# Depthwise convolution of a streaming encoder: products summed by accumulating transfers and turned one chunk later

## The reference

```
hn = rmsnorm(h, norm_mix[0])
u = hn @ w1 + b1;  a, gate = split(u);  u = a * sigmoid(gate)
u = causal depthwise conv(u, w_dw, width 31) + b_dw        # per channel, over positions
u = silu(layernorm(u, ln_g, ln_b)) @ w2 + b2
h = h + u
h = h + sqrelu_mlp(rmsnorm(h, norm_mlp[0]), mlp_w1[0], mlp_w2[0])
# layer 1: multi-scale pooling mixer, then a second MLP; a final rmsnorm
```

## Time and profile before

| | |
|---|---|
| median of three executions | 896.91 us (896.63 to 896.92) |
| profiled execution, its own time | 896.41 us |
| its span, first to last instruction | 894.6 us |
| PE busy | 878.9 us, 98% |
| DVE busy | 704.7 us, 79% |
| ACT busy | 460.5 us, 51% |
| POOL busy | 150.4 us, 17% |
| granted TensorE clock, mean | 0.998 |
| DVE's start of chunk 0 / chunk 7 | 29.91 us / 125.90 us |
| last conv transposes on PE | 139.09 us |

### The profile page before, as it was taken

One profiled execution on the slowest core, in us unless ns is written; L12 is line 12 of the kernel. 1 busy time (PEld: TensorE's weight loads), 2 busy tenths in 40 slices (PEclk: granted clock), 3 DMA queues, 4 the chain that ended last, 5 costly groups with the idle time before them and its releaser, 6 DMA issues.

```text
span 894.6 us, 11948 instructions
## 1 busy us (share of the span) xinstructions
PE 878.9 (98%) x4408; PEld 744.0 (83%) x4408; DVE 704.7 (79%) x948; ACT 460.5 (51%) x666; POOL 150.4 (17%) x127
## 2 busy tenths in 40 slices
PE   8999998999999999999999999999999999999996
PEld 8888876889888888888888889988888888888885
DVE  5899999867977769686868888797776968786856
ACT  5778686255372726344363644637272634436243
POOL 1599993380000020000000051000000000000000
PEclk9999999999999999999999999999999999999999
DMA  9614023305133131423314023123313142331202
GB/s 299 178 50 116 17 79 118 115 27 188 62 128 141 47 141 49 166 81 127 127 61 165 29 92 116 48 63 127 141 47 141 50 165 81 126 131 57 71 1 95
DMA packets 48376, 90.81 MB, mean 102 GB/s; under 512 B 1458, under 2 KB 18866, under 8 KB 48340
## 3 DMA queue, kind: packets, MB, share of 16 engines
q1 hardware_dynamic: 48340, 90.32, 29.1%
HBM read 88.22 MB, written 2.10 MB: 101 GB/s over the span
## 4 chain that ended last, share of the span: by engine, by line
PE 80%; POOL 8%; DVE 6%; DMA 2%; issue 2%; ACT 2%; SPq 0%; POOLq 0%; DVEq 0%; ACTq 0%
PE ps L1365 15%; PE ps L1366 15%; PE ps L1367 15%; PE ps L1599 10%; PE ps L1597 10%; PE ps L1598 10%; POOL w_lo L378 3%; POOL merged_a L388 3%; DMA w_raw<-in_conv_w 2%; POOL merged_b L388 2%; DVE ps L921 2%; PE ps L1384 1%; DVE tok L834 1%; PE ps L1511 1%; PE ps L1516 1%
## 5 line engine op out<-in xcount | busy, mean ns | idle before, releaser
L1365 PE MATMUL ps<-act_hi,w_hi 128*128 128x512 f32 (+1 forms) x704 | 259.8, 369 | 1.1 <-DVE act_lo L840 1.1
L1367 PE MATMUL ps<-act_hi,w_lo 128*128 128x512 f32 (+1 forms) x704 | 258.8, 368 | 0.0
L1366 PE MATMUL ps<-act_lo,w_hi 128*128 128x512 f32 (+1 forms) x704 | 258.8, 368 | 0.0
L1599 PE MATMUL ps<-w_hi,u_lo 128*128 128x512 f32 x392 | 152.7, 390 | 0.0
L1597 PE MATMUL ps<-w_hi,u_hi 128*128 128x512 f32 x392 | 152.7, 389 | 0.0
L1598 PE MATMUL ps<-w_lo,u_hi 128*128 128x512 f32 x392 | 152.5, 389 | 0.0
L1365 PEld LDWEIGHTS ps<-act_hi,w_hi 128*128 128x128 f32 x704 | 132.8, 189 | 23.2 <-DVE act_lo L840 1.4
L1367 PEld LDWEIGHTS ps<-act_hi,w_lo 128*128 128x128 f32 x704 | 132.8, 189 | 22.0
L1366 PEld LDWEIGHTS ps<-act_lo,w_hi 128*128 128x128 f32 x704 | 132.8, 189 | 21.7
L634 ACT ACTIVATE relu<-ps 128x512 f32<-128x512 f32 x36 | 21.5, 597 | 243.0 <-PE ps L1367 243.0
L1102 DVE TENSOR_TENSOR w_lo<-w_raw,w_hi 128x1024 fp32r<-128x1024 f32 x70 | 85.1, 1221 | 58.1 <-ACT w_hi L655 58.1
(11 more groups left out here) (219 smaller groups left out, 1299.1 us busy)
## 6 DMA issues: line engine op xcount, KB each, us to landing
w_raw<-in_mlp_w SPq DMA_DIRECT2D x32, 1024.0 KB, 4.8
w_raw<-in_mlp_w SPq DMA_DIRECT2D x16, 2048.0 KB, 8.0
w_raw<-in_conv_w SPq DMA_DIRECT2D x16, 512.0 KB, 5.6
w_raw<-in_conv_w SPq DMA_DIRECT2D x2, 2048.0 KB, 9.5
h<-in_x SPq DMA_DIRECT2D x4, 512.0 KB, 6.3
out<-tok SPq DMA_DIRECT2D x8, 256.0 KB, 2.2
gain<-in_norm_mix SPq DMA_DIRECT2D x2, 512.0 KB, 6.1
gain<-in_norm_mlp SPq DMA_DIRECT2D x2, 512.0 KB, 6.8
```

Of the source, the lines that this page charges most:

```text
L1365: nc.tensor.matmul(dst, lh, rh, start=(n == 0), stop=False)
L1366: nc.tensor.matmul(dst, lh, rl, start=False, stop=False)
L1367: return nc.tensor.matmul(dst, ll, rh, start=False, stop=(n == count - 1))
L1599: last = nc.tensor.matmul(dst, ll, rh, start=False, stop=(f == 1 and (closes or i not in (0, 5))))
```

## The change

Chunks 0 to 6 are divided anew. ACT makes 14 products instead of 13: nine go into `prod_a` and five into `prod_b` (before, five and eight). POOL adds five products with four adds instead of seven. DVE has 31 - 5 - 9 = 17 taps instead of 18.

The nine products of `prod_a` are no longer turned one by one. They are three groups of three, and two transfers, issued on POOL's queue, add a group onto the first one in SBUF (`accum_op=ALU.add`; source and destination are both `prod_a`, 128 partitions of 1536 float32, 768 KB): `fold_one` adds products 3 to 5, `fold_two` products 6 to 8. Three tiles are left (KEPT), and PE turns them with the merged tile and DVE's sum in `conv_turn(e)`, after `glu_product(e + 2)`; before, the products of chunk e were turned after `glu_product(e + 1)`. The kept group has two places, by the chunk's parity; the other two groups have one place each, so ACT waits before product 3 of a chunk for the last chunk's `fold_one`, and before product 6 for its `fold_two`.

```
-POOL_SHARE = 8
-SHARE = (5, 5, 5, 5, 5, 5, 5, 13)
+POOL_SHARE = 5
+SHARE = (9, 9, 9, 9, 9, 9, 9, 13)
+WIDE = 3
+KEPT = 3
+EARLY = 2 * WIDE
...
+        LAST_SLOT = (6, 7, 8, 3, 4, 5, 9, 10, 11, 0, 1, 2, 6)
+
+        def slot(e, n):
+            if e == NC - 1:
+                return LAST_SLOT[n]
+            return (e % 2) * WIDE + n if n < WIDE else WIDE + n
...
                 if e >= 2:
                     pool.wait_ge(conv_turned, e - 1)
                 into = merged[e % 2]
+                pool.wait_ge(prod_ok, FIRST[e] + EARLY)
+                nc.gpsimd.dma_start(slots(e, 0, WIDE), slots(e, WIDE, WIDE),
+                                    accum_op=ALU.add).then_inc(fold_one[e % 2], 16)
                 for t in range(1, POOL_SHARE):
...
                     add.then_inc(padd_ok, 1)
+                pool.wait_ge(fold_one[e % 2], folds(e))
+                pool.wait_ge(prod_ok, FIRST[e] + SHARE[e])
+                nc.gpsimd.dma_start(slots(e, 0, WIDE), slots(e, 2 * WIDE, WIDE),
+                                    accum_op=ALU.add).then_inc(fold_two[e % 2], 16)
...
+            def products(e):
 
                 act.wait_ge(glu_ok, e + 1)
+                for n in range(SHARE[e]):
+                    if e and n == WIDE:
+                        act.wait_ge(fold_one[(e - 1) % 2], folds(e - 1))
+                    if e and n == 2 * WIDE:
+                        act.wait_ge(fold_two[(e - 1) % 2], folds(e - 1))
+                    product_of(e, n, POOL_SHARE + n)
+                    if n == EARLY - 1:
+                        pool_products(e, range(POOL_SHARE))
+
+            def last_products(which):
+
+                e = NC - 1
+                act.wait_ge(glu_ok, e + 1)
                 for n in which:
+                    if n == 0:
+                        act.wait_ge(fold_one[(e - 1) % 2], folds(e - 1))
+                    if n == 6:
+                        act.wait_ge(fold_two[(e - 1) % 2], folds(e - 1))
+                    if n == RING:
+                        act.wait_ge(prod_read, 1)
+                    product_of(e, n, n)
...
             def conv_turn(e):
+                if e < NC - 1:
+                    if e >= 2:
+                        pe.wait_ge(ctok_ok, e - 1)
                     pe.wait_ge(padd_ok, (POOL_SHARE - 1) * (e + 1))
+                    turn_into(e, merged[e % 2], first=True)
+                    pe.wait_ge(fold_two[e % 2], folds(e))
+                    for n in range(KEPT):
+                        turn_into(e, ring(e, n))
                 pe.wait_ge(conv_ok, e + 1)
...
             for e in range(1, NC):
                 glu_product(e)
-                product_turn(e - 1, range(SHARE[e - 1]))
                 if e >= 2:
                     conv_turn(e - 2)
```

More of the change, by code:

```diff
@@ L183, in hybrid_encoder @@
         cwp_lo_ok, prod_ok, prod_read = sem("cwp_lo_ok"), sem("prod_ok"), sem("prod_read")
+        fold_one = [sem(f"fold_one{k}") for k in range(2)]
+        fold_two = [sem(f"fold_two{k}") for k in range(2)]
         conv_ok, conv_turned, ctok_ok = (sem(n) for n in ("conv_ok", "conv_turned", "ctok_ok"))
@@ L223, in hybrid_encoder, with ring, slots, folds @@
         LAST_TILES = (NQ - 1, 0)
-        def ring(k):
-            return prod_a[:, k % RING, :]
+        LAST_SLOT = (6, 7, 8, 3, 4, 5, 9, 10, 11, 0, 1, 2, 6)
[3 more added lines that the diff above has]
+            return (e % 2) * WIDE + n if n < WIDE else WIDE + n
+        def ring(e, n):
+            return prod_a[:, slot(e, n), :]
+        def slots(e, n, count):
+            return prod_a[:, slot(e, n):slot(e, n) + count, :]
+        def folds(e):
+            return 16 * (e // 2 + 1)
         def pool_ring(k):
@@ L516, in pool_products, with product_of @@
                                          scale=params[:, e, t:t + 1]).then_inc(pprod_ok, 1)
-            def products(e, which):
+            def product_of(e, n, t):
+                nc.scalar.activation(ring(e, n), upad[:, e % 2, t:t + S], ACT.Copy,
+                                     scale=params[:, e, t:t + 1]).then_inc(prod_ok, 1)
+            def products(e):
                 act.wait_ge(glu_ok, e + 1)
-                if pooled_taps(e):
-                    pool_products(e, range(4))
-                for n in which:
[L524 to L531, removed]
+                for n in range(SHARE[e]):
[9 more added lines that the diff above has]
+                act.wait_ge(glu_ok, e + 1)
+                for n in which:
+                    if n == 0:
[5 more added lines that the diff above has]
+                    product_of(e, n, n)
             def c2_high(k):
@@ L551, in _ @@
                     ctok_copy(e - 2)
-                products(e, range(SHARE[e]))
+                products(e)
             gate(NC - 1)
@@ L557, in _ @@
             ctok_copy(NC - 3)
-            products(NC - 1, range(SHARE[NC - 1] // 2))
+            last_products(range(SHARE[NC - 1] // 2))
             c2_high(2)
             ctok_copy(NC - 2)
-            products(NC - 1, range(SHARE[NC - 1] // 2, SHARE[NC - 1]))
+            last_products(range(SHARE[NC - 1] // 2, SHARE[NC - 1]))
             c2_high(3)
@@ L1422, in glu_product, with turn_into @@
                 last.then_inc(glu_mm, 1)
[L1424 to L1434, removed]
+            def turn_into(e, src, first=False, last=False):
+                for b in range(NB):
+                    step = nc.tensor.matmul(ps[:, 4 + e % 2, block_cols(b)], src[:, block_cols(b)], ident[:],
+                                            is_transpose=True, start=(first and b == 0), stop=(last and b == NB - 1))
+                return step
@@ L1436, in conv_turn, with product_turn @@
+            def product_turn(which):
+                e = NC - 1
+                pe.wait_ge(ctok_ok, e - 1)
+                for n in which:
+                    pe.wait_ge(prod_ok, FIRST[e] + n + 1)
+                    turn_into(e, ring(e, n), first=(n == 0)).then_inc(prod_read, 1)
             def conv_turn(e):
-                if pooled_taps(e):
+                if e < NC - 1:
+                    if e >= 2:
+                        pe.wait_ge(ctok_ok, e - 1)
                     pe.wait_ge(padd_ok, (POOL_SHARE - 1) * (e + 1))
-                    for b in range(NB):
-                        nc.tensor.matmul(ps[:, 4 + e % 2, block_cols(b)], merged[e % 2][:, block_cols(b)], ident[:],
-                                         is_transpose=True, start=False, stop=False)
+                    turn_into(e, merged[e % 2], first=True)
+                    pe.wait_ge(fold_two[e % 2], folds(e))
+                    for n in range(KEPT):
+                        turn_into(e, ring(e, n))
@@ L1442, in conv_turn @@
                 pe.wait_ge(conv_ok, e + 1)
                 if e == NC - 1:
[L1444 to L1449, removed]
@@ L1450, in conv_turn @@
-                last.then_inc(conv_turned, 1)
+                    turn_into(e, relu[:, 1 - e % 2, :])
+                turn_into(e, relu[:, e % 2, :], last=True).then_inc(conv_turned, 1)
             def first_upper_half(cols):
@@ L1484, in _ @@
                 glu_product(e)
-                product_turn(e - 1, range(SHARE[e - 1]))
                 if e >= 2:
                     conv_turn(e - 2)
-            product_turn(NC - 1, range(SHARE[NC - 1] // 2))
+            product_turn(range(SHARE[NC - 1] // 2))
             conv_turn(NC - 2)
@@ L1491, in _ @@
                 pe.wait_ge(plast_ok, n + 1)
[L1492 to L1495, removed]
+                turn_into(NC - 1, prod_b[:, n, :])
+            product_turn(range(SHARE[NC - 1] // 2, SHARE[NC - 1]))
             conv_turn(NC - 1)
```

## The result

| | before | changed |
|---|---|---|
| median | 896.77 us (896.21 to 897.59, 6 runs) | 900.34 us (899.23 to 901.27, 6 runs) |
| profiled execution, its own time | 896.41 us | 901.15 us |
| its span | 894.6 us | 899.4 us |
| DVE starts chunk 7 | 125.90 us | 128.71 us |
| DVE's first look at the last conv sums (L940, now L979) | 140.30 us | 145.90 us |

The ratio is 1.0036, interval 1.0026 to 1.0047: the change makes the kernel slower by 0.36%. The forecast was 890.4 us, faster. The sign was wrong; the time is inside the range, near the first rival's 903.

The account below looks back on a forecast made before the run. POOL, PE and DVE were within a microsecond, POOL slowest, DVE setting chunk 7's start. 6.7 us won there less 0.2 at the end made 896.4 - 6.5 = 889.9, plus 0.5 for the median: 890.4 us, range 889.6 to 904.

Parts of the forecast that it names:

- the first rival: Weight load beside fold_one lengthens its landing from 5.4 to 9.3 us; chunk 7 starts 5.7 us later, 903 us; chance 0.25.
- L = 5.4: POOL's queue: time from the end of a fold's issue to its landing, estimated at 5.4 us.
- a round: POOL's cycle per chunk: split 4.60, two issues 2.0, four adds 5.6 us hiding fold_one; 12.2 us, less than DVE's 12.76.
- 85.1 + 5x: Start of chunk 7 on DVE if loads slow fold_one; x is its issue-end-to-landing time, breaking even at 8.2 us.
- D: POOL: the time of one fold issue on its queue, taken as 1.0 us.
- The DVE interference: Each fold issue on POOL stands behind one DVE tap, 1.7 us instead of 1.0; POOL's cycle 13.6 us, time 892.5 us.
- The third rival: Accumulating transfer slow by itself, landing near 8 us even alone; chunk 7 4 us later, about 901 us; chance 0.14.
- The tail: Behind chunk 7's start: chunk 6's copy waits for its fold_two, late by some tenths; 0.2 us given back.
- DVE's step of 12.75: DVE's time per chunk with one tap of 0.66 us fewer, forecast at 12.76 us.
- PE's slack: PE, at 13.1 us per chunk with 8 transposes fewer, stays 2.4 us ahead of DVE at chunk 7.
- taps, waits and PE's transposes: Chunk 7's start on DVE: 4.6 us won from taps, 2.05 from waits; PE's 8 transposes fewer take 0.88 us off a chunk.
- the signs to look for: Forecast wrong if POOL waits for fold_one, rounds exceed 14.5 us, ACT waits before L544 and DVE for the gate.

Follow-up runs that it names:

- experiment 1: Changed kernel without the conv weight loads of chunks 4 to 7, and with the 2 MB load behind the last fold: 889.82 us, ratio 0.9919.
- experiment 4: Changed kernel with plain copies in place of the accumulating transfers, so nothing is added: 889.41 us, ratio 0.9916.
- experiment 11: Changed kernel with filler transposes on PE, 20 in chunk 5's turns and 24 ahead of chunk 7's first turns: 899.50 us, ratio 1.0029.
- 7 and 8: Changed kernel with chunk weight loads behind POOL's second (7) or third (8) add, 2 MB load behind the last fold_two: 889.69 and 889.57 us.

## Why the prediction was wrong

**The step that failed** is POOL's: "so L = 5.4 behind the issue" was used for every fold, and the weight load beside `fold_one` was made a rival with 0.25. The size of a fold alone was right: 5.7 to 6.1 us from issue to landing for a forecast 6.4. What decided was the load, which the prediction had seen to start "the very moment" of the fold. It argued that a fold "may fill gaps that a load from HBM leaves". There are next to none: the load keeps the engines 93% busy for 3.9 us, a fold takes all 16 for 3.93 us, and 5.8 + 3.9 = 9.7 us is what a fold beside a load costs by adding up; 9.0 to 9.8 were measured. So POOL's adds (5.6) didn't hide `fold_one`, and a round was 14.2 to 15.0 us where the sum had 12.2. (The `gain` load, whose issue at 81.06 stands in the earlier trace rows, wasn't in the forecast at all. It falls beside the 9.8, and beside the 7.9 of experiment 1.) The Trainium skill, DMA: Bandwidth & Descriptors, "Issuing engines are not separate DMA queues", says that transfers interleave on the same 16 engines whoever issued them; the trace agrees, with that sum.

**The sum with what was measured.** The split of chunk 7 ends at 107.42 for 97.6 forecast (the first rival: 112.4). `fold_one(5)` then takes 13.0 us (6.6; rival 10.3), `fold_two(5)` 5.7 (6.4; rival 6.4), the products and the gate 2.6 (2.5): 128.7 for 113.1, and 131.6 for the rival. The rival's formula, 85.1 + 5x, gives 128.7 at x = 8.7, but that is luck in part, since its errors cancel. Its fold alone (6.4) and its issue D were too dear: rounds without a load beside them are 11.85 and 12.01 us in experiment 1 (37.65, 49.50, 61.51), which leaves 1.7 to 1.8 for two issues, not 2.0. And it put the same x on chunk 5, where the load is twice as large: by the same adding up, 5.8 + 2.1 MB / 272 GB/s = 13.5; measured 13.0.

**The DVE interference** that would have made D = 1.7 didn't show: POOL began its next instruction at most 0.83 us behind each issue. But the first add behind `fold_one`'s issue steps by 1.5 to 2.0 us where the others take 1.4, and by 1.4 to 1.5 with plain copies (experiment 4), so an accumulating issue costs POOL some tenths more than that. Whether DVE has a part in it is open.

**The third rival,** a fold slow by itself, fell with experiment 1: 5.8 us alone. Yet its suspicion was half right: accumulating doubles the engines' time (experiment 4), and it is that doubling which makes the folds collide. With plain copies the loads stay where they are, `fold_one` of chunk 0 lands in 7.0 us, and the time is that of the kernel without loads.

**The tail** was to be "late by some tenths"; it is 2.8 us. The prediction took the tail as hanging on `fold_two(6)` alone. But `fold_two(5)` was late for PE as well as for ACT (2.0 us of idle PE), chunk 7's late gate holds ACT's casts, its copy and the first of its last products behind it (2.5 us more), and PE's clock falls. PE's first turns of chunk 7 start 1.65 us behind DVE's chunk in the kernel before and 3.10 us behind it in the changed one, with and without fillers: this 1.4 us is ACT's order, and it is what experiment 11's 15.8 us at the full clock holds over 14.4. The other 0.8 to 1.4 go with the clock.

**What was right:** DVE's step of 12.75, PE's slack, POOL's adds of 1.4, its round of 12.2 where no load is beside it (12.3 in chunk 4), that taps, waits and PE's transposes give about 6.5 us when no fold is late (experiments 1, 7 and 8: 889.6 to 889.8 for 890.4), and the signs to look for: POOL waiting behind its adds, ACT before L544, DVE for the gate.

## What to carry to other kernels

When a change puts a transfer on a queue, list what other transfers start in the same microseconds, and add up the time each takes of the DMA engines; a different issuing engine gives no room of its own. An idea that loses for this reason may be saved by a wait that moves the other transfer by a few microseconds. Here a wait that moves the chunk loads by some 3 us made 900.3 into 893.0, and with a second one, for the 2 MB load, it was 889.7. A gate placed too late (behind the landing) gives part of it back, since the moved transfer meets the next one.

## What was not expected of the hardware

- An accumulating transfer within SBUF takes the DMA engines twice as long as the copy of the same bytes: 3.93 against 1.97 us for 768 KB, 5.8 against 3.9 us to landing. Its row on POOL is 0.85 to 1.17 us long, the copy's mostly 0.57.
- The sharing goes both ways: the 512 KB loads land in 7.3 us beside folds for 4.8 in the kernel before, the 2 MB load in 13.9.
- After PE idled 2.03 us following a steady stretch at 2.4 GHz, the granted clock was at the 1.2 GHz level from about 127 to 137 us, though transposes kept PE busy from 132 us on; after 2.06 us of idle at 94 us it was there from about 96 to 99.5 us. In the kernel before PE idled 1.66 us ahead of the same transposes of chunk 7, and the clock stayed at 1.00.
